# A page-score search on 16-bit keys, and the scaling of the softmax rows divided between two engines

## The reference

```
s     = einsum('bqhd,bsd->bqhs', qi, ki) * IDX_DIM ** -0.5        # indexer, 8 heads
score = einsum('bqhs,bqh->bqs', relu(s), wi * IDX_HEADS ** -0.5)
_, idx = lax.top_k(score, topk)      # 128 of 512 keys for a prompt token, 256 of 2049 for a sample token
p = softmax(q . k[idx] * HEAD_DIM ** -0.5);   o = p @ v[idx]      # 16 heads, 4 key heads
```

## Time and profile before

| | |
|---|---|
| median of 3 runs | 1841.1 us (1838.33 to 1841.72) |
| the profiled execution | 1841.42 us, of it 1839.6 us span |
| mean granted TensorE clock | 0.989 of full |
| PE busy | 1767.8 us, 96% |
| DVE busy | 1452.0 us, 79% |
| ACT busy | 931.7 us, 51% |
| POOL busy | 422.6 us, 23% |

### The profile page before, as it was taken

One profiled execution on the slowest core, in us unless ns is written; L12 is line 12 of the kernel. 1 busy time (PEld: TensorE's weight loads), 2 busy tenths in 40 slices (PEclk: granted clock), 3 DMA queues, 4 the chain that ended last, 5 costly groups with the idle time before them and its releaser, 6 DMA issues.

```text
span 1839.6 us, 36078 instructions
## 1 busy us (share of the span) xinstructions
PE 1767.8 (96%) x14199; PEld 1694.6 (92%) x14199; DVE 1452.0 (79%) x2177; ACT 931.7 (51%) x1464; POOL 422.6 (23%) x312
## 2 busy tenths in 40 slices
PE   7999999999998798999999999999999899999997
PEld 7999999987975498999999989999999799999996
DVE  5988887675988537988887598888876898888875
ACT  4455563353358726555562275555523565556333
POOL 3100044262220545000043230000543320002430
PEclk9999999999999999999999999999999999999998
DMA  5663423236210241334323324333233223433231
GB/s 170 191 201 95 114 87 104 87 100 141 53 56 1 67 136 52 104 103 114 94 89 100 108 69 115 102 103 115 87 96 105 59 62 99 113 107 99 83 102 47
DMA packets 275473, 180.74 MB, mean 98 GB/s; under 512 B 9366, under 2 KB 271902, under 8 KB 274845
## 3 DMA queue, kind: packets, MB, share of 16 engines
q1 hardware_dynamic: 266071, 158.50, 30.1%
q0 software_dynamic: 2144, 13.04, 2.0%
q10 hardware_dynamic: 7150, 7.70, 1.8%
HBM read 169.56 MB, written 8.08 MB: 97 GB/s over the span
## 4 chain that ended last, share of the span: by engine, by line
PE 74%; DVE 15%; ACT 6%; issue 3%; DMA 1%; POOL 0%; SPq 0%; ACTq 0%; DVEq 0%; POOLq 0%
PE ps L1371 41%; PE ps L1250 15%; PE ps L1434 9%; PE ps L1494 2%; DVE w_lo L1954 2%; PE ps L1499 1%; DVE q_lo L2639 1%; ACT xh L749 1%; ACT xf L751 1%; ACT p_t L886 1%; PE ps L1271 1%; DVE w_lo L2532 1%; ACT sc L864 1%; DVE q_sum L2716 1%; DVE xf L2004 1%
## 5 line engine op out<-in xcount | busy, mean ns | idle before, releaser
L2803 POOL TENSOR_TENSOR hl<-hid_all,hh 128x520 fp32r<-128x520 f32 x56 | 98.1, 1783 | 748.5 <-ACT hh L1110 748.5
L1040 ACT CAST w_hi<-w_sum 128x1024 fp32r<-128x1024 f32 x160 | 167.9, 1050 | 114.6 <-DVE w_sum L2514 107.2
L2532 DVE TENSOR_TENSOR w_lo<-w_sum,w_hi 128x1024 fp32r<-128x1024 f32 x160 | 194.6, 1218 | 4.5 <-ACT w_hi L1040 4.5
L1250 PE MATMUL ps<-hh,w_hi 128*128 128x260 f32 x896 | 191.6, 284 | 2.0 <-DVE w_lo L1954 2.0
L1250 PE MATMUL ps<-hh,w_lo 128*128 128x260 f32 x896 | 189.1, 282 | 0.0
L1371 PE MATMUL ps<-t_hi,w_hi 128*128 128x260 f32 x640 | 161.6, 284 | 0.7 <-DVE w_lo L2532 0.3
L1371 PE MATMUL ps<-xh,w_hi 128*128 128x260 f32 x640 | 159.9, 282 | 0.8 <-DVE w_lo L2532 0.8
L1371 PE MATMUL ps<-t_hi,w_lo 128*128 128x260 f32 x640 | 160.7, 283 | 0.0
L1371 PE MATMUL ps<-xh,w_lo 128*128 128x260 f32 x640 | 159.5, 283 | 0.0
L1250 PEld LDWEIGHTS ps<-hh,w_hi 128*128 128x128 f32 x896 | 145.3, 188 | 2.9 <-issue 2.7
L1250 PEld LDWEIGHTS ps<-hh,w_lo 128*128 128x128 f32 x896 | 145.6, 188 | 0.2
(11 more groups left out here) (375 smaller groups left out, 5235.9 us busy)
## 6 DMA issues: line engine op xcount, KB each, us to landing
w_raw<-in_ffn_wi_dram SPq DMA_DIRECT2D x176, 512.0 KB
w_raw<-in_ffn_wo_dram SPq DMA_DIRECT2D x16, 1024.0 KB
w_raw<-in_ffn_wo_dram SPq DMA_DIRECT2D x32, 512.0 KB
w_raw<-in_ffn_wo_dram SPq DMA_DIRECT2D x16, 768.0 KB
w_raw<-in_attn_w_in_dram SPq DMA_DIRECT2D x8, 1024.0 KB
keys_scratch<-key_half POOLq DMA_DIRECT2D x2, 2048.0 KB, 8.5
w_raw<-in_attn_w_o_dram SPq DMA_DIRECT2D x4, 1024.0 KB
x_in<-in_x_prompt_dram ACTq DMA_DIRECT2D x4, 512.0 KB, 9.8
```

Source lines behind the costliest of these rows:

```text
L1040: nc.scalar.copy(blocks(st, j)[1][0][:, x], w_sum[:, c % 2, x]).then_inc(s_sums_hi, 1)
L1250: mm = nc.tensor.matmul(ps[0:mc, bank + 2 * m + h, 0:HT], w[:, k, m, 0:mc], x(k)[:, h * HT:(h + 1) * HT], start=first and k == 0 and w is ...
L2532: nc.vector.tensor_tensor(lo[:, x], w_sum[:, (st.chunk + j) % 2, x], hi[:, x].bitcast(F32), ALU.subtract).then_inc(s_sums_lo, 1)
L2803: nc.gpsimd.tensor_tensor(hl[:, k, :], hid_all[:, k, :], hh[:, k, :].bitcast(F32), ALU.subtract).then_inc(s_hl, 1)
```

## The change

Two edits.

The search works on 16-bit keys. `ordered` turns the fp32 scores into 32-bit integers of the same order and takes the upper half of each as `key`. Six steps (`SHIFTS` 13, 10, 7, 4, 1, 0) find the upper half of the threshold; `low_keys` then makes a new 16-bit key from the lower half (held at the ends of the range where the upper half differs), six more steps find the lower half, and `threshold` puts the two together again. `test` compares int16 with int16 and writes bf16 in the order [7, page, token]; the step's weight is multiplied in when the counts are read, so `take` has two instructions, L2207's and L2210's, and there is no `delta` nor an update of `thr`. There are 12 tests and no count of signs; the number of side steps is the same.

In blocks 0 to 7 (`SHARED` is 8) VectorE scales rows 0 and 1, straight behind the reciprocal in `inverse`, and ScalarE rows 2 and 3. TensorE waits for VectorE's rows on a semaphore of their own, `s_p_dve`.

```diff
-STEPS = (28, 25, 22, 19, 16, 13, 10, 7, 4, 1, 0)
-UNITS_OF = len(STEPS)
+SHIFTS = 2 * (13, 10, 7, 4, 1, 0)
+UNITS_OF = len(SHIFTS)
+HIGH_UNITS = UNITS_OF // 2
...
-    unit = np.array([[j << u if u or j == 1 else 0 for j in range(1, 8)] for u in STEPS], np.int32).reshape(1, -1)
-    out["unit"] = np.tile(unit.view(np.float32), (P, 1))
+    out["unit"] = np.tile(np.array([[j << u if u else 1 for j in range(1, 8)] for u in SHIFTS], f).reshape(1, -1), (P, 1))
...
-        tests = at("tests", [P, NC, DEC, 7], BF16)
+        tests = at("tests", [P, 7, NC, DEC], BF16)
...
+        cand = at("cand", [P, 7, DEC], I16)
+        reach = at("reach", [P, 2, DEC, 8])
+        half_thr = at("half_thr", [P, 2, DEC])
+        order = at("order", [P, DEC, NC])
+        order_sign = at("order_sign", [P, DEC, NC], I32)
+        key = at("key", [P, NC, DEC], I16)
+        distance = at("distance", [P, NC, DEC])
...
-        SIDES = UNITS_OF + 4
+        SIDES = UNITS_OF + 3
...
+        SHARED = LATE - N_KV
...
-                for r in range(4):
+                first = 2 if B < SHARED else 0
+                for r in range(first, 4):
                     e = nc.scalar.activation(attn(B, r)[:, 0:n], attn(B, r)[:, 0:n], ACT.Copy, scale=row_inv[:, B % 2, r:r + 1])
                     if r % 2 == 1:
-                        e.then_inc(s_p, 1)
+                        e.then_inc(s_p, 1 + first // 2)
...
-                                mm = nc.tensor.matmul(ps[:, 6, 0:DEC * 7], ones_bf[:], tests[:, c].rearrange("p b j -> p (b j)"),
+                                mm = nc.tensor.matmul(ps[:, 6, 0:DEC * 7].rearrange("p (j b) -> p j b", b=DEC), ones_bf[:], tests[:, :, c, :],
                                                       start=c == 0, stop=c == NC - 1)
...
-                            if j == 0 and r % 2 == 0:
+                            if j == 0 and r == 0 and B < SHARED:
+                                pe.wait_ge(s_p_dve, B + 1)
+                            elif j == 0 and r % 2 == 0:
                                 pe.wait_ge(s_p, 2 * B + r // 2 + 1)
...
+                def ordered():
+
+                    bits, order_i = order[:].bitcast(I32), order_sign[:]
+                    step(nc.vector.memset(reach[:, 0, :, 0], -32768.0))
+                    done(step(nc.vector.tensor_scalar(order[:], scores, 0.0, None, ALU.add)))
+                    done(step(nc.vector.tensor_scalar(order_i, bits, 31, 1, ALU.arith_shift_right, ALU.logical_shift_right)))
+                    done(step(nc.vector.tensor_tensor(bits, bits, order_i, ALU.bitwise_xor)))
+                    done(step(nc.vector.tensor_scalar(bits, bits, 32768, None, ALU.bitwise_xor)))
+                    done(step(nc.vector.tensor_copy(key[:], half_keys(1))))
+
+                def half_keys(part):
+
+                    return order[:].bitcast(I16).rearrange("p b (n t) -> p n b t", t=2)[:, :, :, part]
+
                 def test(k):
 
-                    units = cst("unit")[:, 7 * k:7 * k + 7].bitcast(I32)
-                    n = step(nc.vector.tensor_tensor(cand[:], thr[:].unsqueeze(2).broadcast_to([P, DEC, 7]),
-                                                     units.unsqueeze(1).broadcast_to([P, DEC, 7]), ALU.bitwise_xor))
-                    done(n)
-                    nc.vector.tensor_tensor(tests[:], scores.rearrange("p b n -> p n b").unsqueeze(3).broadcast_to([P, NC, DEC, 7]),
-                                            cand[:].bitcast(F32).unsqueeze(1).broadcast_to([P, NC, DEC, 7]), ALU.is_ge)\
-                      .then_inc(s_hits, 1)
+                    units = cst("unit")[:, 7 * k:7 * k + 7].unsqueeze(2).broadcast_to([P, 7, DEC])
+                    done(step(nc.vector.tensor_tensor(cand[:], reach[:, k % 2, :, 0].unsqueeze(1).broadcast_to([P, 7, DEC]), units, ALU.add)))
+                    nc.vector.tensor_tensor(tests[:], key[:].unsqueeze(1).broadcast_to([P, 7, NC, DEC]),
+                                            cand[:].unsqueeze(2).broadcast_to([P, 7, NC, DEC]), ALU.is_ge).then_inc(s_hits, 1)
 
                 def take(k):
 
-                    widths = 7 if STEPS[k] else 1
-                    dve.wait_ge(s_cnt, k + 2)
-                    at_ = step(nc.vector.tensor_scalar(reach[:], ps[:, 6, 0:DEC * 7].rearrange("p (b j) -> p b j", b=DEC), float(TOPK_D),
-                                                       None, ALU.is_ge))
-                    done(at_)
-                    at_ = step(nc.vector.tensor_reduce(need[:], reach[:, :, 0:widths], AX.X, ALU.add))
-                    done(at_)
-                    at_ = step(nc.vector.tensor_tensor(delta[:], need[:], cst("unit")[:, 7 * k:7 * k + 1].bitcast(I32).broadcast_to([P, DEC]),
-                                                       ALU.mult))
-                    done(at_)
-                    at_ = step(nc.vector.tensor_tensor(thr[:], thr[:], delta[:], ALU.bitwise_xor))
-                    done(at_)
+                    widths = 7 if SHIFTS[k] else 1
+                    new = half_thr[:, k // HIGH_UNITS, :] if SHIFTS[k] == 0 else reach[:, (k + 1) % 2, :, 0]
+                    dve.wait_ge(s_cnt, k + 1)
+                    done(step(nc.vector.tensor_scalar(reach[:, k % 2, :, 1:8], ps[:, 6, 0:DEC * 7].rearrange("p (j b) -> p b j", b=DEC),
+                                                      float(TOPK_D), float(1 << SHIFTS[k]), ALU.is_ge, ALU.mult)))
+                    done(step(nc.vector.tensor_reduce(new, reach[:, k % 2, :, 0:1 + widths], AX.X, ALU.add)))
+
+                def low_keys():
+
+                    step(nc.vector.memset(reach[:, 0, :, 0], -32768.0))
+                    done(step(nc.vector.tensor_tensor(distance[:], key[:], half_thr[:, 0, :].unsqueeze(1).broadcast_to([P, NC, DEC]),
+                                                      ALU.subtract)))
+                    done(step(nc.vector.scalar_tensor_tensor(distance[:], distance[:], 65536.0, half_keys(0), ALU.mult, ALU.add)))
+                    done(step(nc.vector.tensor_scalar(key[:], distance[:], 32767.0, -32768.0, ALU.min, ALU.max)))
+
+                def threshold():
+
+                    halves_of = thr[:].bitcast(I16).rearrange("p (b t) -> p b t", t=2)
+                    step(nc.vector.tensor_copy(halves_of[:, :, 1], half_thr[:, 0, :]))
+                    done(step(nc.vector.tensor_copy(halves_of[:, :, 0], half_thr[:, 1, :])))
+                    done(step(nc.vector.tensor_scalar(thr[:], thr[:], 32768, None, ALU.bitwise_xor)))
+                    done(step(nc.vector.tensor_scalar(thr_sign[:], thr[:], 31, 1, ALU.arith_shift_right, ALU.logical_shift_right)))
+                    done(step(nc.vector.tensor_tensor(thr[:], thr[:], thr_sign[:], ALU.bitwise_xor)))
 
                 def side(n):
 
                     if n == 0:
                         dve.wait_ge(s_rw, DEC + 1)
-                        nc.vector.tensor_scalar(hits[:], scores, 0.0, None, ALU.is_ge).then_inc(s_hits, 1)
-                    elif n == 1:
-                        counted(0)
-                        done(step(nc.vector.tensor_scalar(thr[:], need[:], float(TOPK_D), -1.0, ALU.is_lt, ALU.mult)))
+                        ordered()
                         test(0)
-                    elif n <= UNITS_OF:
-                        take(n - 2)
-                        test(n - 1)
-                    elif n == UNITS_OF + 1:
+                    elif n < UNITS_OF:
+                        take(n - 1)
+                        if n == HIGH_UNITS:
+                            low_keys()
+                        test(n)
+                    elif n == UNITS_OF:
                         take(UNITS_OF - 1)
-
+                        threshold()
                         t = by_column(thr[:].bitcast(F32))
                         step(nc.vector.tensor_tensor(above[:], scores, t, ALU.is_gt))
                         step(nc.vector.tensor_tensor(equal[:], scores, t, ALU.is_equal))
                         nc.vector.tensor_tensor(hits[:], scores, t, ALU.is_gt).then_inc(s_hits, 1)
...
                 nc.vector.reciprocal(row_inv[:, B % 2, :], row_sum[:, B % 2, :]).then_inc(s_rinv, 1)
+                if B < SHARED:
+                    dve.wait_ge(s_rinv, B + 1)
+                    n = (BLOCKS[B][0] + 1) * P
+                    for r in range(2):
+                        x = nc.vector.tensor_scalar(attn(B, r)[:, 0:n], attn(B, r)[:, 0:n], row_inv[:, B % 2, r:r + 1], None, ALU.mult)
+                    x.then_inc(s_p_dve, 1)
 
```

More of the change, by code:

```diff
@@ L12 @@
 BF16 = mybir.dt.bfloat16
+I16 = mybir.dt.int16
 ALU = mybir.AluOpType
@@ L127, in at @@
         def at(name, shape, dt=F32, offset=None):
-            size = int(np.prod(shape[1:])) * (2 if dt == BF16 else 4)
+            size = int(np.prod(shape[1:])) * (2 if dt in (BF16, I16) else 4)
             if offset is None:
@@ L281, in trunk_kernel @@
         top[0] = kidx_off
-        tests = at("tests", [P, NC, DEC, 7], BF16)
+        tests = at("tests", [P, 7, NC, DEC], BF16)
```

(27 more changed lines are left out.)

## The result

The change makes the kernel slower: 1846.06 us (1844.17 to 1848.86, nine runs) against 1840.6 (1837.97 to 1841.72, nine runs). The forecast was 1845.2. Only runs in the chip's usual state are compared; one execution of a later experiment (the comparison twice in even sides) was in the slower state, took 1934 us and is left out.

A forecast was written before the change was run, and what follows sets the result against it. A once-a-block ring through VectorE, TensorE and ScalarE was taken to bound the edited stretch, not one full engine. Terms -3.6 + 1.0 + 0.5 + 1.5 + 0.6 + 0.3 + 1.7 + 2.1 gave +4.1: 1845.2 us median, range 1843.5 to 1847.5.

The forecast's parts named there:

- Ring and int16 rate: Even side steps: int16 comparison 0.65 us for 1.15, `take` 0.40 less; sides 4, 6, 8, 10 gain 0.90 each, -3.6 us.
- The rival of the fp32 rate: The int16 comparison gains no speed: 0.50 us more on sides 0, 2, 4, 6, 8, 10; +3.0, 1848.2; chance 0.10.
- The odd sides: Odd side steps fill VectorE's second half of a block, which waits for the exponentials anyway: gain nothing.
- `low_keys`, `threshold`: New search work on even sides: `low_keys` in side 6 costs +1.0 us; side 12 with `threshold` costs +0.5 us net.
- The start: Side 0's conversion waits out GpSimd's rotation, ending 3.2 us later; +1.5 us by side 2's comparison, +0.6 for TensorE coming late.
- ScalarE costs nothing: Two rows fewer in each of eight blocks save ScalarE 9 us, none on the ring; costed at nothing.
- the cover named: ScalarE's wait for TensorE's transposes, ten times 1.8 us, 1.3 without the longest, taken to hide its saving.
- VectorE's rows: Scaled rows ahead of `out_low`: hidden in blocks 0 to 3, out by 0.15 us in passes for blocks 7, 8; +0.3.
- The fills: GpSimd's fills hold up VectorE's second scaled row: +1.7 us at `count` (block 2), +2.1 at `q_pad` (block 5).
- The rival in which row 1 goes first: VectorE's row 1 runs ahead of GpSimd's fills: 3.8 us go, leaving +0.3, 1841.4; chance 0.20.
- The clock rival: TensorE's clock falls again in the two stalls at GpSimd's fills: +2.5 us, 1847.7; chance 0.12.
- the ring: Once-a-block chain through VectorE, TensorE and ScalarE, 8.02 us at 384 keys, claimed to bound the prompt attention between 528 and 610 us.

The follow-up runs named there:

- the search alone: The changed kernel with all four rows scaled by ScalarE again, so only the search is new; ratio 1.0004, +0.7 us against the kernel before.
- the fills later: The changed kernel with GpSimd's two fills waiting for VectorE's scaled rows of the same block; ratio 1.0017, +3.1 us against the kernel before.
- the two-tensor run: The changed kernel, VectorE scaling rows of block 0 alone, score conversion in two-tensor instructions; ratio 1.0003, +0.6 us against the kernel before.
- the scaling alone: The kernel before with its old search, VectorE scaling rows 0 and 1 of blocks 0 to 7; ratio 1.0035, +6.4 us.
- row maxima ahead of side 0: The changed kernel, VectorE scaling block 0 alone, both pairs of block 1's row maxima before side step 0; ratio 1.0007, +1.3 us against the kernel before.
- TensorE's order: As row maxima ahead of side 0, with TensorE doing block 2's scores before side 0, block 0's values between sides 0 and 1; ratio 1.0001, +0.2 us.

## Why the prediction was right

- **Ring and int16 rate.** The comparison takes 653 ns against the 0.65 assumed, `take` is two instructions shorter, and sides 4, 6, 8 and 10 gain 0.85 to 0.92 each, with 0.90 forecast. The rival of the fp32 rate is out. Whether the 16-bit type alone gives the rate, or the new order of `tests` has a part in it, is not shown. The odd sides are free but for 0.5 us in sides 1 and 3.
- **`low_keys`, `threshold`.** +1.0 (0.13 + 0.9) and +0.48, for +1.0 and +0.5.
- **The start.** Side 0 ends 3.3 us late behind the rotation (3.2 forecast). Counted from the mask, side 2's comparison ends at 23.25 for 21.53 before, 1.7 us late where 1.5 was forecast, and the start of `out_high` in the pass for block 3 is +2.66 for +2.1. The term that was mis-sized is the search's own: the expectation for the search alone gave 0.6 of the 2.1 to the scaled rows and left 1.5 for the search, but the search alone has 2.11, and the scaled rows add 0.55. In that run the clock is at 0.50 from 536 to 546 us, in the kernel before until 542. How much of the 0.6 is clock is not separated.
- **ScalarE costs nothing.** Right for seven blocks. Its saving was 7.7 us and not 9. Wrong for block 0, where the cover named, the wait for the transposes, does not exist: there two rows fewer give 1.4 us in the old search. In the changed kernel the late first count swallows them: the reciprocal of block 1 comes 19.37 us behind the mask, and 19.40 in the search alone. The step that failed took an average over ten waits for a first block with another order of work.
- **VectorE's rows.** 0.15 in the pass for block 5 of the changed kernel, 0.12 and 0.10 in those for blocks 7 and 8 with the fills later, for 0.15 in each of the last two. Block 5's was not forecast.
- **The fills.** 2.6 us for the two rows (2.7 by the forecast's times); `count` cost 1.60 for 1.7, `q_pad` 1.94 (1.09 + 0.85) for 2.1. The rival in which row 1 goes first is out. The rule quoted from the Trainium skill (SBUF — State Buffer, "Who interferes with whom") held at both fills in the five kernels that share the rows of eight blocks: with the fills in place the second row waits (2.59 and 2.62 us), with the fills later `neg_max` does. The same section says that an instruction with two inputs in SBUF contends with a GpSimd instruction that reads SBUF, and that a reduction on this chip never does; the two-tensor run agrees with both (0.73 and 1.32 held up, 0.29 not).
- **The clock rival.** It was not an alternative but a further term, and came true at one of the two stalls: 1.2 us in the pass up to side 12 (1.78, against 0.60 with the fills later and the clock at 1.00). I had priced it at 2.5 for both and left it out of the sum. In the scaling alone it was 1.6, behind the other stall. Why one stall of a kernel lowers the clock and the other does not is open.

With 0.6 for the start and 1.2 for the clock my sum would be 5.9, beside 5.74 measured up to side 14, 5.4 for the stretch and 6.6 (5.2 to 8.1) for the whole time. So the mechanism was right where the loss lies, in the fills, and 1845.2 came 0.9 us below the median because two terms, the clock and the search's part of the start, were too small. That it came so near has some luck in it: with the clock lowered behind both stalls, at these two prices of 1.6 and 1.2, the sum would be 7.5, by this estimate.

## What to carry to other kernels

Moving work to another engine pays only where the engine it leaves is the one that is waited for. Price each engine's time by its place in the ring (here full price in an even side, hardly any in an odd one, and for ScalarE only in the first block, where the order differs). Before giving VectorE an elementwise instruction in SBUF, list what GpSimd starts in that window, and what the same event releases on both. And a stall of 2 us on TensorE's supplier can have a second price, the slow clock behind it. Here it came at one of two stalls, for 1.2 and 1.6 us in two kernels, so it belongs in the sum with its chance, and not among the rivals.

## What the runs showed of the hardware

- An int16 comparison of two broadcast operands with bf16 out took 653 ns for 952 elements, where the bf16 row gave an estimate of 0.65 us; the fp32 one, in another order of elements, took 1150.
- A fill that is moved behind one VectorE instruction catches the next small one: `neg_max` took 0.54, 0.69 and 0.96 us instead of 0.17 (0.23 and 0.26 in the kernel before), while row maxima out of PSUM beside the same fills kept their 0.55 and 0.68.
- After idle times of 2.9 us (the change) and 3.2 us (row maxima ahead of side 0) TensorE's first count ran at the lower clock (0.97 us), after 2.08 (TensorE's order) at the full one (0.61). At the second stall the kernel that had idled longer (1.63 and 1.50 us, the scaling alone) kept its full clock, and the one that had idled less (1.64 and 0.65, the change) lost it, so the idle time of the stall alone did not tell.
- Stages with the same code ahead of the attention took 522.9 to 525.5 us in the profiled executions of fourteen kernels. The spans of the two profiles show +3.1 us, about half of this change's loss.
